# The sums of a Strassen step in a one-core decoder layer: from VectorE to GpSimd, with a longer ring and more steps

## The reference, cut to what matters

```python
h = h + mix                                  # the attention block
u = rms_norm(h, norm_mlp_g[i])
h = h + jnp.square(jax.nn.relu(u @ mlp_w1[i])) @ mlp_w2[i]
gate = jax.nn.sigmoid(rms_norm(h, ple_norm_g[i]) @ ple_w_gate[i])
h = h + gate * (p[i] @ ple_w_proj[i])
```

## Time and profile before

| | |
|---|---|
| median of 3 runs | 1185.96 us (1185.25 to 1186.37) |
| profiled execution | 1186.18 us; its span, first to last instruction, 1184.4 us |
| PE busy | 1176.9 us, 99% of the span |
| DVE, ACT, POOL busy | 827.9, 635.5, 22.5 us |
| mean granted clock | 0.999 of full speed |

### The profile page before, as it was taken

One profiled execution on the slowest core, in us unless ns is written; L12 is line 12 of the kernel. 1 busy time (PEld: TensorE's weight loads), 2 busy tenths in 40 slices (PEclk: granted clock), 3 DMA queues, 4 the chain that ended last, 5 costly groups with the idle time before them and its releaser, 6 DMA issues.

```text
span 1184.4 us, 14269 instructions
## 1 busy us (share of the span) xinstructions
PE 1176.9 (99%) x5417; PEld 978.0 (83%) x5417; DVE 827.9 (70%) x1141; ACT 635.5 (54%) x882; POOL 22.5 (2%) x31
## 2 busy tenths in 40 slices
PE   9999999999999999999999999999999999999998
PEld 7888888888888888888888888888888888888886
DVE  5568876888776667755788755879655888676554
ACT  6745455666656565543565543456533566455443
POOL 1000100000000000000000000000000000000000
PEclk9999999999999999999999999999999999999999
DMA  9867663333348665865477865476854577886661
GB/s 341 322 178 242 215 235 139 108 108 134 109 162 281 210 215 199 279 233 194 146 244 250 273 214 191 176 247 232 285 195 178 192 243 241 273 258 208 217 207 44
DMA packets 110980, 249.26 MB, mean 210 GB/s; under 512 B 9664, under 2 KB 55744, under 8 KB 110912
## 3 DMA queue, kind: packets, MB, share of 16 engines
q1 hardware_dynamic: 110768, 248.34, 61.9%
q10 hardware_dynamic: 144, 0.01, 0.0%
...
## 4 chain that ended last, share of the span: by engine, by line
PE 99%; DMA 0%; DVE 0%; SPq 0%; ACT 0%; issue 0%
PE acc L1786 59%; PE acc L1812 11%; PE tr L1812 7%; PE sc L1786 7%; PE sc L1812 6%; PE sc L2013 1%; PE sc L1978 1%; PE tr L1930 1%; PE tr L1919 0%; PE sc L1919 0%; PE tr L2066 0%; PE tr L2065 0%; DMA w_raw<-in_nsa_w_in_units_dram 0%; PE acc L1902 0%; PE tr L2042 0%; PE tr L2043 0%
## 5 line engine op out<-in xcount | busy, mean ns | idle before, releaser
L1176 DVE TENSOR_TENSOR w_split<-w_raw,w_split 128x1024 fp32r<-128x1024 f32 x296 | 358.7, 1220 | 211.6 <-ACT w_split L733 210.9
L733 ACT ACTIVATE w_split<-w_raw 128x1024 fp32r<-128x1024 f32 x296 | 309.7, 1057 | 255.3 <-PE acc L1786 194.3
L1786 PE MATMUL acc<-w_split,b_split 128*128 128x512 f32 x1536 | 355.3, 390 | 0.0
L1786 PEld LDWEIGHTS acc<-w_split,b_split 128*128 128x128 f32 x1536 | 287.3, 188 | 59.1
L1786 PE MATMUL acc<-w_split,a_hi 128*128 128x512 f32 x1020 | 318.1, 393 | 1.6 <-DVE w_split L1172 1.6
L1786 PEld LDWEIGHTS acc<-w_split,a_hi 128*128 128x128 f32 x1020 | 188.6, 188 | 40.9 <-issue 2.4
L1786 PE MATMUL acc<-w_split,a_lo 128*128 128x512 f32 x510 | 198.9, 390 | 0.0
L744 ACT ACTIVATE w_split<-w_raw 128x1024 fp32r<-128x1024 f32 x95 | 97.6, 1052 | 44.4 <-PE acc L1786 20.9
L1190 DVE TENSOR_TENSOR w_split<-w_raw,w_split 128x1024 fp32r<-128x1024 f32 x78 | 93.3, 1217 | 31.3 <-ACT w_split L744 31.3
L1786 PEld LDWEIGHTS acc<-w_split,a_lo 128*128 128x128 f32 x510 | 95.7, 188 | 20.3
L1812 PE MATMUL acc<-w_split,a_hi 128*128 128x512 f32 x298 | 91.7, 389 | 0.0
...
## 6 DMA issues: line engine op xcount, KB each, us to landing
w_raw<-in_mlp_w_units_dram SPq DMA_DIRECT2D x256, 512.0 KB, 4.4
w_raw<-in_nsa_w_in_units_dram SPq DMA_DIRECT2D x76, 512.0 KB, 4.6
w_raw<-in_nsa_w_out_units_dram SPq DMA_DIRECT2D x32, 512.0 KB, 4.2
w_raw<-in_ple_w_gate_units_dram SPq DMA_DIRECT2D x32, 512.0 KB, 4.3
...
```

The costliest lines, as they stand in the source:

```text
L733: nc.scalar.activation(w_hi[:, u % SPLIT], w_raw[:, u % RAW], ACT.Copy).then_inc(hi_done, 1)
L1176: nc.vector.tensor_tensor(w_lo[:, u % SPLIT], w_raw[:, u % RAW], f32(w_hi[:, u % SPLIT]), ALU.subtract).then_inc(lo_done, 1)
L1786: last = nc.tensor.matmul(banks_of(c)[t][:], xs[:, kt, toks], ws[:, u % SPLIT, m * NW:(m + 1) * NW], start=(kt == 0 and n == 0), stop=(kt ...
```

## The change

1. The four sums move to GpSimd, which writes them to a buffer of their own, `t_raw` (t1 and t3 in its first half, t2 and t4 in the second). It waits for both raw units, and for the lo parts of the last step's sums before it overwrites them. `w_raw` is no longer changed; SP waits for the sums (`sums`) before it loads over either unit.
2. `w_split` and `t_split` become one ring of six places, four plus two. Everything that is split, a unit or a pair of sums, is an **item** and takes the next place in order (`ITEM`, `T_ITEM`, `place`, `place_free`). A Strassen step has four items: two units (the second one with half of its columns) and two pairs of sums. The ring is six places from the first Strassen step to the end of the kernel.
3. `QUADS = (2, 3, 4, 5, 6)` in all seven couples: 7 x 5 = 35 Strassen steps. The combined tokens grow from 128 x 1536 to 128 x 2560 elements.
4. PE waits four times in a Strassen step, once for each item, and takes the products in another order.
5. To make room, buffers are laid out anew: the blocks to be turned and the turned blocks share `v_slc` and `v_win`, so DVE waits for `turned_split` before a transpose, and `keep_one` does too. The transposed token columns of `p` are loaded and split at the end of the MLP and not at its start. Several small steps move by one to three places in the lists `s in (...)`.

```diff
-QUADS = (2, 4, 6)
+QUADS = (2, 3, 4, 5, 6)
 def quads(c):
-    return QUADS if (c - C_MLP) % 8 == 0 else QUADS[1:]
+    return QUADS
...
+WIDER = ITEM[QUAD_UNITS[0]]
+PLACES = (SPLIT, SPLIT + 1, *((WIDER + n) % SPLIT for n in range(SPLIT)))
+def place(item):
+    return item % SPLIT if item < WIDER else PLACES[(item - WIDER) % len(PLACES)]
+def place_free(item):
+    if WIDER <= item < WIDER + len(PLACES) - SPLIT:
+        return 0
+    return item + 1 - (SPLIT if item < WIDER else len(PLACES))
...
-                    sp.wait_ge(lo_done, raw_free(u - RAW))
+                    sp.wait_ge(lo_done, ITEM[u - RAW] + 1)
+                    for v in (u - RAW, u - RAW - 1):
+                        if v in QUAD_UNITS:
+                            sp.wait_ge(sums, 4 * QUAD_UNITS.index(v) + 4)
...
+            pool.wait_ge(r_done, 1)
+            t1, t3, t2, t4 = (t_raw[:, m // 2, m % 2 * NW:(m % 2 + 1) * NW] for m in range(4))
+            for at, u in enumerate(QUAD_UNITS):
...
+                for v in (u, u + 1):
+                    pool.wait_ge(raw_full[v % RAW], 16 * (v // RAW + 1))
+                if at:
+                    pool.wait_ge(sums, 4 * at)
+                    pool.wait_ge(lo_done, T_ITEM[QUAD_UNITS[at - 1]][0] + 1)
+                nc.gpsimd.tensor_tensor(t1, b11, b12, ALU.add).then_inc(sums, 1)
+                nc.gpsimd.tensor_tensor(t3, b12, b22, ALU.add).then_inc(sums, 1)
+                if at:
+                    pool.wait_ge(lo_done, T_ITEM[QUAD_UNITS[at - 1]][1] + 1)
+                pool.wait_ge(sums, 4 * at + 1)
+                nc.gpsimd.tensor_tensor(t2, t1, b22, ALU.add).then_inc(sums, 1)
+                pool.wait_ge(sums, 4 * at + 3)
+                nc.gpsimd.tensor_tensor(t4, t2, b21, ALU.add).then_inc(sums, 1)
...
+                    if u - 1 in QUAD_UNITS:
+                        place_hi(ITEM[u], w_raw[:, u % RAW, NW:UW], NW)
+                        for m, item in enumerate(T_ITEM[u - 1]):
+                            act.wait_ge(sums, 4 * QUAD_UNITS.index(u - 1) + 2 * (m + 1))
+                            place_hi(item, t_raw[:, m])
...
-                    dve.wait_ge(direct, at + 1)
-                    nc.vector.tensor_tensor(b11, b11, b12, ALU.add).then_inc(first_sums, 1)
-                    dve.wait_ge(first_sums, 2 * at + 1)
-                    nc.vector.tensor_tensor(b12, b12, b22, ALU.add).then_inc(first_sums, 1)
...
+                        place_lo(ITEM[u], w_raw[:, u % RAW, NW:UW], NW)
+                        for m, item in enumerate(T_ITEM[u - 1]):
+                            place_lo(item, t_raw[:, m])
...
+                if n >= T_H1 + 2:
+                    dve.wait_ge(turned_split, n - 1)
```

More of the change, by code:

```diff
@@ L127, with _number_items @@
 QUAD_UNITS = [FIRST[c] + 2 * k for c in PAIR_NO for k in quads(c)]
-QUADS_TO = {c: sum(len(quads(b)) for b in PAIR_NO if b <= c) for c in PAIR_NO}
-def raw_free(u):
-    return u + 2 if u in QUAD_UNITS else u + 1
+UNITS = FIRST[C_PLE] + 4 * (1 + UPC)
+ITEM, T_ITEM = {}, {}
+def _number_items():
+    n = 0
+    for u in range(UNITS + 1):
+        ITEM[u] = n
+        n += 1
+        if u - 1 in QUAD_UNITS:
+            T_ITEM[u - 1] = (n, n + 1)
+            n += 2
+    return n
+N_ITEMS = _number_items()
+END.update({c: ITEM[u] for c, u in END.items() if c >= C_MLP})
+WIDER = ITEM[QUAD_UNITS[0]]
[6 more added lines that the diff above has]
+    return item + 1 - (SPLIT if item < WIDER else len(PLACES))
 T_KS, T_KW, T_H1 = range(3)
@@ L391, in pair_banks, with weights @@
             return tr + mlp_acc[1], mlp_acc[0] + sc
+        def weights(item):
+            n = place(item)
+            return (x[:, n % SPLIT] for x in ((w_hi, w_lo) if n < SPLIT else (t_hi, t_lo)))
         def quad_tiles(x, n):
@@ L1708, in down_pair @@
                 for s in split_lo(FIRST[c + 2], 2 * UPC):
-                    if s == 0 and q:
-                        turned_hidden(1, q)
-                    if s == 2:
+                    if s == 3:
                         pair_sums(c)
-                    if s in (4, 6):
+                    if s in (5, 7):
                         turn_hidden(n + s // 2 - 2)
@@ L1832, in quad @@
                 u = FIRST[c] + 2 * k
-                at = QUAD_UNITS.index(u)
-                def split(x, v, m):
-                    return tuple(y[:, v, m * NW:(m + 1) * NW] for y in x)
+                own, rest = (ITEM[u], ITEM[u + 1]), T_ITEM[u]
                 def combined(r):
                     return tuple(x[:, r, i] for x in (r_hi, r_lo))
-                own, sums_of = (w_hi, w_lo), (t_hi, t_lo)
                 start, stop = k == quads(c)[0], k == quads(c)[-1]
@@ L1844, in quad @@
                 one, five, six, seven = mixes
[L1845 to L1847 removed]
+                pe.wait_ge(lo_done, own[0] + 1)
+                product(one, tile_rows(2 * k, 0), split(own[0], 0), start, stop)
+                product(c11, tile_rows(2 * k + 1, 0), split(own[0], 1), False, False).then_inc(unit_used, 1)
+                pe.wait_ge(lo_done, own[1] + 1)
                 pe.wait_ge(r_done, 1)
[L1849 to L1854 removed]
+                product(c12, combined(3), split(own[1], 1), False, False).then_inc(unit_used, 1)
+                pe.wait_ge(lo_done, rest[0] + 1)
+                product(five, combined(0), split(rest[0], 0), start, stop)
+                product(seven, combined(2), split(rest[0], 1), start, stop).then_inc(unit_used, 1)
+                pe.wait_ge(lo_done, rest[1] + 1)
+                product(six, combined(1), split(rest[1], 0), start, stop)
+                product(c21, tile_rows(2 * k + 1, 1), split(rest[1], 1), False, False).then_inc(unit_used, 1)
             def up_pair(q, p):
```

212 lines of the change are left out of this document (91 added, 121 removed).

## The result

The changed kernel takes 1264.57 us (median of 4 runs, 1262.78 to 1265.87), the one before 1186.13 beside it: a ratio of 1.066, 95% interval 1.064 to 1.068. It is 78.4 us slower. Forecast were 1240.0 us, a range of 1185 to 1284 and slower at 0.79; sign and range held, and the median lies 24.6 us above the forecast.

What follows compares the result with a forecast made beforehand. PE was taken to bound the kernel, busy 99% of the span. From 1186.2 us, 12.2 of saved matmuls were taken off and 66 of losses in seven couples added: 1240 us, range 1185 to 1284.

Steps and rivals of the forecast that it cites:

- PE's saving: On PE: 18 more steps become Strassen steps, each 4.76 instead of 5.44 us, 12.2 us less.
- The parts at nothing: SP's wait for sums, the wait for turned_split, the longer combined-token input, PE's extra waits, moved split of p: no cost.
- Who holds the input: DVE's two-input subtractions and GpSimd's adds exclude each other at SBUF: 8.54 us a Strassen step against PE's 4.76; chance 0.68.
- Rival A: GpSimd's stream of adds meets no contention, so all 12.2 us are kept: 1174 us; chance 0.12.
- rival B: GpSimd waits for DVE but not the reverse; 17 us lost in seven couples: 1191 us; chance 0.17.
- Rival C: The sums are made early, in plain steps, so contention falls where there is slack; no size or chance of its own.
- The add's length: A GpSimd add of 128 x 512 takes 1.10 us with hand-over, bounds 0.69 and 1.57; four are 4.4 us.
- The loss in a couple: PE waits for late lo parts in the Strassen steps of a couple: 9.5 us each, 66 in seven.
- What is stored up: Six ring places hold one and a half steps; j = 2 is 1.4 us late, j = 3 5.2, j = 4 9.0.
- the forecast's chain: The walk through sums, ACT's copy and DVE's lo parts in a couple, ending with j = 4 9.0 us late.
- a lower clock in the gaps: PE's clock falling where it waits; named with a stall at a couple's end as something unforeseen, together 0.03, no size.

Runs made afterwards that it cites:

- idle adds: The kernel before, with four extra GpSimd adds per Strassen step on a tile that nobody reads and nothing waits for: 1231.88 us, ratio 1.039.
- both runs with 28 steps: The changed kernel with Strassen steps 2, 3, 5, 6 in all couples: 1218.01 us with all adds on GpSimd, 1203.91 with t1, t3 on DVE.
- the shared one with 24: The changed kernel with four Strassen steps in p = 0 couples, three in p = 1; t1, t3 on DVE, t2, t4 on GpSimd: 1191.88 us.
- idle fills: The kernel before, with eight extra GpSimd fills per Strassen step on a tile that nobody reads and nothing waits for: 1185.62 us, ratio 1.000.
- 21 on DVE: The changed kernel with 21 Strassen steps and the four adds on DVE: 1186.43 us; with t1 and t3 joined in one add: 1185.81 us.

## Why the prediction was right, and where it was short

**PE's saving, 12.2 us: right.** With fills in place of adds the whole kernel takes 1174.73, forecast 1174.0 for a kernel in which nothing else matters. The parts at nothing are confirmed by the same run, to about 1 us.

**Who holds the input: right, in both directions.** The step from one row (GpSimd 0.9 us late behind DVE) to the reverse was argued, from reads of 8 elements, and is now shown: from 1.23 to 2.30 us for a lo part in the kernel after, from 0.69 to 1.51 for a half one in the kernel before with idle adds. Rival A (no contention, 1174) and rival B (one-sided, 1191) fall. DVE is held, and a one-sided account has no place for the 46 us of the idle adds. Rival C falls by the matmuls, 54 fewer, and by the adds' places in the couples.

**The add's length: 1.10 us taken, right for what it was needed for.** The measured add lies between its bounds: one alone is shown with 1.27 us, two in a row start 1.23 to 1.25 apart, less than three accesses in a row would take (1.57). It holds the input for less than it lasts: a lo part and an add in turn take 2.26 us together, and 1.14 is the lo part's, so some 1.12 are the add's. The Trainium skill ("GPSIMD Engine Reference", Performance versus the Vector engine) gave an estimate of 1.12 us for the whole add. The measured duration of 1.27 is 0.15 longer; the hold, which is what the sum needed, happens to be as long as the estimate. The forecast's period for a step was 8.54 us, the measured one 8.5 to 8.7.

**The loss in a couple: 9.5 us forecast, 13.1 measured (91.5 / 7).** This is the term that was mis-sized, the part "What is stored up". It priced one kind of couple. The seven, cut where PE turns from one to the next, are of three kinds. The second pair:

```profile
773.14:823.06 49.92, 42.48 (x178) 32.60 (x177) 39.60 (x30) 24.58 (x27) 35.21 (x19) 1.00 0.36 128
823.06:879.76 56.70, 46.38 (x178) 34.12 (x177) 50.36 (x41) 30.56 (x38) 33.60 (x18) 0.94 0.57 185
```

| couples | us | lost, over 40.1 | forecast |
|---|---|---|---|
| first, `p` = 1 | 55.4 | 15.3 | 9.5 |
| three of `p` = 0 | 51.5, 49.9, 51.5 | 11.4, 9.8, 11.4 | 28.5 |
| three of `p` = 1 | 53.5, 56.7, 53.8 | 13.4, 16.6, 13.6 | 28.5 |

1. *The first couple, 5.8 us over.* The sum let the sums of j = 0 and 1 be ready when PE comes to them, and the first late step be j = 2. But GpSimd stands at its first add until `r_done`:

```profile
439.33 2.21 POOL L742 TENSOR_TENSOR t_raw<-w_raw 128x512 f32<-128x512 f32 x1 [38.82 <-DVE r_split L1725]
```

PE's couple starts at 438.46, so nothing is stored up, and PE's first wait comes in j = 1:

```profile
457.39 1.66 PE L1850 MATMUL acc<-t_split,r_split 128*128 128x512 f32 x6 [1.09 <-DVE t_split L1239]
```

The list of GpSimd's instructions in the section on the change shows `r_done` at this add. It didn't enter the sum. A subtraction of `turned_hidden` (2.32 us at 440.30, held by an add) and two transposes lie in this couple too; the shares of the 5.8 us were not measured.

2. *The `p` = 0 couples, 4.1 us over in three.* The one at 773.14 keeps its clock at 1.00 and loses 9.8, where the forecast's chain ends at 9.0 for a couple without `turned_hidden`. This is the forecast's mechanism undisturbed, right to 0.8 us. The other two have the same last wait and then the lower clock:

```profile
1009.78:1014.23 4.45, 4.45 (x12) 3.49 (x13) 3.46 (x4) 2.49 (x4) 1.61 (x2) 0.62 0.88 292
```

12 matmuls in 4.45 us instead of 2.72 are 1.7 us, and 11.4 - 9.8 = 1.6. The prediction had "a lower clock in the gaps" among the unforeseen. In the middle of a couple it is hidden: 992.73 to 997.22 has 12 matmuls in 4.49 us too, but PE would have waited for the next lo part anyway.

3. *The `p` = 1 couples, 15.1 us over in three.* These carry the transposes and `turned_hidden`. The forecast gave the latter one undisturbed subtraction in a couple. But it stands ahead of j = 4's own lo parts and is itself held by an add:

```profile
1055.03 2.33 DVE L1338 TENSOR_TENSOR b_split<-v_win,b_split 128x1024 fp32r<-128x1024 f32 x1
1057.27 3.98 DVE L1239 TENSOR_TENSOR w_split<-w_raw,w_split 128x1024 fp32r<-128x1024 f32 x2
```

It takes 2.24 us from start to start (the couple's second one, 1.22 us, comes when the last sum is through), and PE's longest wait, 2.70 us, ends on the lo part behind it. Transposes, 1.3 us for two, lie in the stretch too and are in no term of the sum. In the couple at 823.06 the low clock lasts on, with 10 matmuls from 868 to 873 us at a granted clock of 0.50. How the 15.1 us divide among these was not measured; that this kind of couple is the tight one is what both runs with 28 steps and the shared one with 24 show.

The sum with the measured hold of 1.12 us in place of 1.10 gives about 1242 us. The range reached up to 1284 because an add might have held the input for 1.57, which it didn't. That 1264.57 lies in the range is in part luck: a width set for one term took in the error of another.

**A simpler sum would have come as near**, with 7 x (49.9 - 40.1) = 68.6 us for the 66 of the forecast. Per `p` = 0 couple the input is needed for 5 x 8.62 + 3 x 2.27 = 49.9 us with five Strassen steps (measured 49.92 at full clock), 4 x 8.62 + 4 x 2.27 = 43.6 with four (43.28 at full clock), and 37.2 with three, under PE's 41.48 (41.48). That five steps agree to 0.02 us is chance: the sum takes the input to be busy all the time, but for some 4.7 us of this couple neither a lo part nor an add runs. The longest such time in the stretch lies between the end of an add (813.72) and a lo part that waits for ACT's copy, and PE waits for that lo part:

```profile
811.57 2.15 POOL L749 TENSOR_TENSOR t_raw<-t_raw,w_raw 128x512 f32<-128x512 f32 x1
...
814.84 1.23 DVE L1239 TENSOR_TENSOR w_split<-t_raw,w_split 128x1024 fp32r<-128x1024 f32 x1 [2.27 <-ACT w_split L795]
```

So the chain of sum, copy and lo part has a share in the loss beside the reads, as the forecast's walk had it too. A second buffer for the sums, which might loosen it, was not tried.

**The expectations of the runs** went the same way. Where one mechanism was switched, they held (fills, idle adds, idle fills; adds on DVE within 4 us). Where a balance of 1% decided, they missed: 1187 expected and 1185 measured for 17 steps, 1188 and 1182 for 21, 1184 and 1186 and then 1183 and 1186 for 21 on DVE, 1202 and 1218, 1184 and 1204 for 28, 1187 and 1192, 1180.5 and 1192 for 24.
